# A two-layer decoder kernel: attention probabilities turned a step later, and half of layer 1's memory keys computed between the layers and a quarter inside layer 0's router

## The chip, the cores and the metric

The kernel runs on one core of a Trainium2 chip. The metric is device time in microseconds (us) for one call, the lower the better; the median of three runs stands for the kernel.

The engines are TensorE (PE in the profile; its weight loads are PEld), VectorE (DVE), ScalarE (ACT), GpSimd (POOL) and SyncE (SP), which issues the weight loads. Each runs its own list of instructions in order, and they wait for each other by semaphores.

## The reference, cut to what matters

Two layers (L = 2) over 256 tokens of width 1024, all in float32. In each layer:

```python
mix = hybrid_mixer(x, positions, w_in[l], ...)          # 4 latent + 6 forgetting + 6 dilated heads
x = layer_norm(ALPHA * x + mix, ln_mix_g[l], ln_mix_b[l])
# memory_cross_attention, 4 heads of 256:
q = to_heads(x @ xattn_w_q[l])
k, v = split(mem @ xattn_w_kv[l], 2)                    # mem doesn't depend on x or l
x = layer_norm(ALPHA * x + softmax(q k^T / 16) v @ xattn_w_o[l], ...)
gates = shared_group_router(x, router_w, router_bias)   # one group of four, two experts of it
x = layer_norm(ALPHA * x + moe_ffn(x, gates, ...))      # 16 experts
```

The memory keys are `mem @ xattn_w_kv[l][:, 0:1024]`. They depend on the memory and on the layer's weights alone, so they can be computed at any time before the cross-attention of their layer.

## The kernel before, in words

**Weights.** All weights come in one fixed order, `weight_stream` (L53): 168 blocks ("subs") for each layer, each of 128 partitions and up to 1024 elements. SyncE loads block i into a ring of 12 raw slots (L451) once VectorE is through with block i - 12. ScalarE writes the high part of the block into one of 4 slots, `split_hi` (L500, L504), after TensorE has freed that slot; VectorE writes what is left, `split_lo` (L506, L509). A product of TensorE is three matmuls: high by high, high by low, low by high (L1557 to L1559). A block of keys (`columns`, L1592) is 24 matmuls of 256 columns; a block of width 512 (`rows`, L1578) is 12 of 512 columns, one of the input projections 12 of 384 to 416.

**Jobs and banks.** Every projection is a job with a pair of PSUM banks (table at L276). A job may open when the job that held its pair is evacuated (L1569). A is the latent projection, FQ, FK, FV the forgetting heads, DQ, DK, DV the dilated heads, UQ and UKV the second latent step, MK0 and MK1 the memory keys (feature chunks 0 to 3 and 4 to 7), MV0 and MV1 the memory values, WO0 and WO1 the output projection, XQ, XO the cross-attention's projections, RT the router, U and D the experts.

**The head loop.** After UKV, `for s in range(HEADS + 3)` (PE L1975, ACT L858, DVE L1408) runs 19 steps over 16 heads. `slots` (L405) deals the 29 blocks from FQ's third to WO0's third over the steps. In step s the engines do, each in this order:

- TensorE: the blocks of step s; the value products of heads s-4 and s-3 together (even s from 4); turn head s-2's probabilities; scores of head s-1; turn queries and keys of head s.
- ScalarE: high halves for the blocks of step s+1; copies of finished jobs (DK, MK0, MK1 and others); copy of queries and keys of head s (L732); exponentials of head s-1 (L746); high part of the output (L754).
- VectorE: low halves for the blocks of step s+1 (L509); copies of DV and MV0 (L1047); scaled and masked scores with their maximum, and nmx (L1063, L1066), of head s-1; copy of the turned probabilities of head s-2 (L1097); sum's reciprocal and normalised probabilities of head s-1 (L1085, L1089; dilated heads are weighted by dilcount first, L1082); low part of the output (L1107).

The last six heads (dilated) go in pairs: scores and maxima of two heads in every second step. p_sb and pT have two slots. GpSimd rotates dq and dk in the early steps (L600 to L606); in layer 0 it builds the dilated masks before.

**Between the layers.** At the end of layer 0 TensorE adds up the experts' outputs (`scatter`, L1864). VectorE then adds and normalises token tile 0 and tile 1 (L1144, L1161). TensorE turns each tile when it is ready. In the meantime it runs fill matmuls whose result nobody reads (`keep_busy`, L1657): 20, then 5, then 11 (L1917, L1923, L1933). ScalarE and VectorE split the first two blocks of A ahead of that.

**The router.** After the cross-attention TensorE scores the tokens. It runs 6 fill matmuls while it waits for tile 1 (L2058), then 11 in `gather` (L1814) while VectorE picks the groups (L1207), ending in `ing` (L1233), and 2 more before the selected tokens are gathered.

## Time and profile before

| what | value |
|---|---|
| median of 3 runs | 820.36 us (818.98 to 822.27) |
| profiled execution, its own time | 822.08 us |
| span of the profiled execution | 820.5 us |
| mean granted TensorE clock | 0.990 |
| PE busy | 797.2 us, 97% |
| PEld busy | 688.0 us, 84% |
| DVE busy | 634.1 us, 77% |
| ACT busy | 508.5 us, 62% |
| POOL busy | 78.4 us, 10% |
| read from HBM | 175.18 MB, 215 GB/s over the span |
| chain that ended last | PE 81%, DVE 10%, ACT 4%, issue 2%, DMA 2% |

The span goes from the first to the last instruction. A matmul counts as busy from its start to the end of its drain, and the next one starts before that end; so the distance of two starts is what a matmul costs in a dense row, and not its own duration. In a row of the timeline the first number is the start, the second the time to the end of the last instruction that the row merges (x2: two of them), and a bracket names the idle time before and what ended it.

### The profile page before, as it was taken

To read this page: it belongs to the slowest core of one execution; us is meant where nothing else is said; L and a number is where in the kernel's file an instruction comes from. 1 tells how busy PE (TensorE), PEld (TensorE's weight loads), DVE (VectorE), ACT (ScalarE), POOL (GpSimd) and SP (SyncE) were. 2 spreads that over 40 slices of the span, in tenths; PEclk is the share of its full clock that TensorE was granted. 3 is DMA by queue.
4 is the path that set the end of the run, shared out by engine and by line. 5 is a ranking of instruction groups with operands and counts; after the bars stand their busy time and mean duration, and the time that the engine had idled before them with its cause. 6 is when DMAs were issued, how large, how long until landed. Compare 5 with 4: busy or idle time off the path is not lost.

```text
span 820.5 us, 12140 instructions
## 1 busy us (share of the span) xinstructions
PE 797.2 (97%) x4364; PEld 688.0 (84%) x4364; DVE 634.1 (77%) x1110; ACT 508.5 (62%) x804; POOL 78.4 (10%) x150
## 2 busy tenths in 40 slices
PE   7899999999999999999999999999999999999995
PEld 7899897789877888888899989877998788888884
DVE  5657868785658999999765586786846699999995
ACT  4755554554546788888555555554454567888873
POOL 3148200020000000000011350000200000000000
PEclk9999999999999999999999999999999999999998
DMA  8954443475334799999755644336643439999951
GB/s 289 344 182 155 144 135 130 139 228 157 105 126 134 246 368 367 364 370 374 259 150 146 209 142 154 105 129 204 209 129 99 145 120 342 367 369 364 370 209 52
DMA packets 122095, 177.06 MB, mean 216 GB/s; under 512 B 10177, under 2 KB 90577, under 8 KB 122033
## 3 DMA queue, kind: packets, MB, share of 16 engines
q1 hardware_dynamic: 120048, 169.56, 62.0%
q0 software_dynamic: 1984, 6.70, 2.9%
q8 instruction: 36, 0.59, 0.3%
q14 instruction: 27, 0.21, 0.1%
HBM read 175.18 MB, written 1.05 MB: 215 GB/s over the span
## 4 chain that ended last, share of the span: by engine, by line
PE 81%; DVE 10%; ACT 4%; issue 2%; DMA 2%; SPq 0%; POOL 0%; DVEq 0%; ACTq 0%; POOLq 0%
PE bank L1557 22%; PE bank L1559 22%; PE bank L1558 22%; DVE w_split L509 3%; DMA raw<-in_w_in_dram 2%; PE bank L1660 2%; PE bank L1724 2%; PE bank L1765 2%; PE bank L1870 2%; DVE xg_lo L1496 1%; ACT w_split L504 1%; PE bank L1756 1%; PE bank L1735 1%; PE bank L1713 1%; PE bank L1785 1%
## 5 line engine op out<-in xcount | busy, mean ns | idle before, releaser
L509 DVE TENSOR_TENSOR w_split<-raw,w_split 128x1024 fp32r<-128x1024 f32 (+3 forms) x336 | 386.0, 1173 | 69.8 <-ACT w_split L504 63.6
L504 ACT ACTIVATE w_split<-raw 128x1024 fp32r<-128x1024 f32 (+3 forms) x336 | 335.4, 1010 | 103.7 <-PE bank L1559 86.2
L1557 PE MATMUL bank<-w_split,xg_hi 128*128 128x512 f32 x256 | 102.9, 402 | 0.0
L1559 PE MATMUL bank<-w_split,xg_lo 128*128 128x512 f32 x256 | 100.1, 391 | 0.0
L1558 PE MATMUL bank<-w_split,xg_hi 128*128 128x512 f32 x256 | 99.9, 390 | 0.0
L1557 PE MATMUL bank<-w_split,xT_hi 128*128 128x384 f32 (+2 forms) x224 | 77.9, 348 | 3.1 <-DVE w_split L509 2.3
L1559 PE MATMUL bank<-w_split,xT_lo 128*128 128x384 f32 (+2 forms) x224 | 76.5, 341 | 0.0
L1558 PE MATMUL bank<-w_split,xT_hi 128*128 128x384 f32 (+2 forms) x224 | 76.2, 340 | 0.0
L1559 PEld LDWEIGHTS bank<-w_split,xg_lo 128*128 128x128 f32 x256 | 48.0, 188 | 10.3
L1557 PEld LDWEIGHTS bank<-w_split,xg_hi 128*128 128x128 f32 x256 | 48.1, 188 | 9.5 <-DVE xg_lo L1496 0.6
L1558 PEld LDWEIGHTS bank<-w_split,xg_hi 128*128 128x128 f32 x256 | 48.2, 188 | 9.0
L1557 PE MATMUL bank<-w_split,mixT_hi 128*128 128x512 f32 x128 | 51.9, 405 | 2.0 <-DVE w_split L509 1.9
L1559 PE MATMUL bank<-w_split,mixT_lo 128*128 128x512 f32 x128 | 50.0, 391 | 0.0
L1558 PE MATMUL bank<-w_split,mixT_hi 128*128 128x512 f32 x128 | 50.0, 390 | 0.0
L1559 PE MATMUL bank<-w_split,aT_lo 128*128 128x512 f32 x128 | 49.8, 389 | 0.0
L1557 PE MATMUL bank<-w_split,aT_hi 128*128 128x512 f32 x128 | 49.8, 389 | 0.0
L1558 PE MATMUL bank<-w_split,aT_hi 128*128 128x512 f32 x128 | 49.8, 389 | 0.0
L732 ACT ACTIVATE qkT<-bank 66x512 f32<-66x512 f32 (+2 forms) x26 | 15.5, 595 | 53.4 <-PE bank L1693 39.6
L1557 PEld LDWEIGHTS bank<-w_split,xT_hi 128*128 128x128 f32 x224 | 42.7, 191 | 4.3 <-issue 2.6
L1558 PEld LDWEIGHTS bank<-w_split,xT_hi 128*128 128x128 f32 x224 | 42.6, 190 | 0.2
L1559 PEld LDWEIGHTS bank<-w_split,xT_lo 128*128 128x128 f32 x224 | 42.5, 190 | 0.1
L746 ACT ACTIVATE p_sb<-p_sb,nmx 128x128 f32<-128x128 f32 x64 | 28.6, 447 | 19.1 <-DVE nmx L1066 18.8
(314 smaller groups left out, 1550.9 us busy)
## 6 DMA issues: line engine op xcount, KB each, us to landing
raw<-in_expert_w_gate_dram SPq DMA_DIRECT2D x128, 256.0 KB, 5.8
raw<-in_expert_w_up_dram SPq DMA_DIRECT2D x128, 256.0 KB, 7.8
raw<-in_expert_w_down_dram SPq DMA_DIRECT2D x64, 512.0 KB, 7.8
raw<-in_xattn_w_kv_dram SPq DMA_DIRECT2D x32, 512.0 KB, 4.1
raw<-in_w_in_dram SPq DMA_DIRECT2D x40, 384.0 KB, 4.0
raw<-in_w_mix_out_dram SPq DMA_DIRECT2D x16, 512.0 KB, 3.8
raw<-in_xattn_w_q_dram SPq DMA_DIRECT2D x16, 512.0 KB, 3.4
raw<-in_xattn_w_o_dram SPq DMA_DIRECT2D x16, 512.0 KB, 5.5
```

Source lines behind the costliest of these rows:

```text
L504: nc.scalar.activation(w_hi[:, i % SPL, 0:w], raw[:, i % RAW, 0:w], ACT.Copy).then_inc(hi_ready, 1)
L509: nc.vector.tensor_tensor(w_lo[:, i % SPL, 0:w], raw[:, i % RAW, 0:w], w_hi[:, i % SPL, 0:w].bitcast(F32), ALU.subtract).then_inc(lo_ready, 1)
L732: nc.scalar.activation(qkT[0:d, qk_slot(h), :], B_QK[0:d, :], ACT.Copy).then_inc(qkT_ready.sem, n)
L746: nc.scalar.activation(p_sb[:, h % 2, sl], src, ACT.Exp, bias=nmx[:, h, t:t + 1], scale=scale, accum_out=acc[:, h, t:t + 1]).then_inc(e_re ...
L1496: nc.vector.tensor_tensor(xg_lo[:, f, :, :].rearrange("p g s -> p (g s)"), bank[XG_BANKS[f]][:, :], xg_hi[:, f, :, :].rearrange("p g s -> ...
L1557: nc.tensor.matmul(o, lhs[0], rhs[0], start=first, stop=False, skip_group_check=shared)
L1558: nc.tensor.matmul(o, lhs[0], rhs[1], start=False, stop=False, skip_group_check=shared)
L1559: return nc.tensor.matmul(o, lhs[1], rhs[0], start=False, stop=last, skip_group_check=shared)
L1660: nc.tensor.matmul(bank[7][:, :], ones[:, :], memT_hi[:, 0:2, :].rearrange("p k t -> p (k t)"), start=True, stop=True)
L1724: ins = nc.tensor.matmul(o[:, t * T:(t + 1) * T], qTx[:, 2 * g + c_, t * P:(t + 1) * P], kTx[:, 2 * g + c_, :], start=c_ == 0, stop=c_ == 1)
L1765: ins = nc.tensor.matmul(value_bank(h)[:, dblk * T:(dblk + 1) * T], vx[:, c_, f * P:(f + 1) * P], pT[:, h % 2, c_ * T:(c_ + 1) * T], start ...
L1870: ins = nc.tensor.matmul(bank[2 * t + h][:, :], selT[:, g, t * P:(t + 1) * P], v[:, g, 512 * h:512 * h + 512], start=g == 0 and v is y_hi, ...
```

## The change

1. **Probabilities turned a step later.** The head loop has 20 steps. TensorE turns head s-3's probabilities in step s and makes the value products from step 5 on. VectorE's order in a step becomes: low halves; normalise head s-2; copy of the turned probabilities of s-3; maxima of s-1; output. Three slots of probabilities (`probs`) and two of turned ones take the place of p_sb and pT. The exponentials of dilated heads no longer write their sums.
2. **Layer 1's keys.** MK0 and MK1 exist in layer 0 only. In layer 1 ME1 (4 blocks, keys' chunks 4 to 7) stands between the layers in place of the 36 fill matmuls. MH0 (2 blocks, chunks 0 and 1) is computed into bank 7 in layer 0's router in place of the 6 and the 11 fills; its split parts have a buffer of their own (`early`), so it takes no turn in the ring of 4. The result is kept in `kept` and copied into kTx in layer 1. MH1 (2 blocks, chunks 2 and 3) stays in layer 1's head loop.
3. `slots` is a list for each layer: layer 0 gets one step more with one block, layer 1 has 23 blocks, one a step after the first two steps. ScalarE and VectorE split ME1 ahead at the end of layer 0, in place of two blocks of A. UKV uses bank pair 1, and from MV0 on layer 1 swaps pairs 0 and 1.

Cut to its core (index and signature changes that follow from it are left out):

```diff
@@ weight_stream @@
+        if l:
+            subs += [(l, "ME1", j) for j in range(4)]
...
-                         ("MK0", range(4)), ("MK1", range(4)), ("MV0", range(4)), ...
+                         ("MK0", range(0 if l else 4)), ("MK1", range(0 if l else 4)), ("MH1", range(2 if l else 0)), ("MV0", range(4)), ...
...
+            if name == "RT" and l + 1 < n_layers:
+                subs += [(l + 1, "MH0", 0)]
             subs += [(l, name, j) for j in js]
+            if name == "RT" and l + 1 < n_layers:
+                subs += [(l + 1, "MH0", 1)]
@@ build @@
-        slots = [3, 2, 2] + [2, 1] * 4 + [1, 2] * 2 + [1] * 4
+        slots = [[3, 2, 2] + [2, 1] * 4 + [1, 2] + [1] * 7] + [[3, 2] + [1] * 18] * (L - 1)
...
+        def free_turns(h):
+            return h - 2 if h < HEADS else max(h - 1, HEADS)
...
+            if i in turn_of:
+                act.wait_ge(split_free, slot_freed(i))
+            nc.scalar.activation(halves_of(i)[0][:, 0:w], raw[:, i % RAW, 0:w], ACT.Copy).then_inc(hi_ready, 1)
@@ scalar @@
-                if h >= 2:
-                    act.wait_ge(pt_done.sem, pt_done.at(l, h - 1))
+                if h >= 3:
+                    act.wait_ge(pt_done.sem, pt_done.at(l, free_turns(h)))
...
-                if l == 0:
-                    split_hi(act, first)
+                split_hi(act, first)
                 turn_x(l, "XT0", 0)
...
+                if l:
+                    act.wait_ge(split_free, free_at(index[l, "UKV", 0]))
+                    nc.scalar.activation(kTx[:, 0:2, :], kept[:, :, :], ACT.Copy).then_inc(keys_moved.sem, 1)
+                    keys(l, "ME1", 4)
...
                 for j in range(2):
                     split_hi(act, index[l, "RT", j])
+                if l + 1 < L:
+                    split_hi(act, index[l + 1, "MH0", 1])
...
+                if l + 1 < L:
+                    wait_job(l + 1, "MH0")
+                    nc.scalar.activation(kept[:, :, :], bank[7][:, :].rearrange("p (c t) -> p c t", c=2), ACT.Copy)\
+                        .then_inc(early_kept.sem, 1)
...
                 if l + 1 < L:
-                    for j in range(2):
-                        split_hi(act, index[l + 1, "A", j])
+                    for j in range(3):
+                        split_hi(act, index[l + 1, "ME1", j])
                 y_of(l, NG - 1)
+                if l + 1 < L:
+                    split_hi(act, index[l + 1, "ME1", 3])
@@ vector @@
-                for s in range(HEADS + 3):
+                for s in range(HEADS + VALUED):
                     for i in ahead_of[l][s]:
                         split_lo(dve, i)
...
+                    if 2 <= s < HEADS + 2:
+                        softmax_norm(l, s - 2)
+                    if TURNED <= s < HEADS + TURNED:
+                        evac_pT(l, s - TURNED)
                     for h in scored(s):
                         softmax_max(l, h)
-                    if in_pair(s - 1) and s % 2 == 0:
-                        softmax_norm(l, s - 1)
-                    if 2 <= s <= HEADS + 1:
-                        evac_pT(l, s - 2)
-                    if 1 <= s <= HEADS and not (in_pair(s - 1) and s % 2 == 0):
-                        softmax_norm(l, s - 1)
...
                 split_lo(dve, index[l, "XO1", 3])
+                if l + 1 < L:
+                    split_lo(dve, index[l + 1, "MH0", 0])
...
                 for j in range(2):
                     split_lo(dve, index[l, "RT", j])
+                if l + 1 < L:
+                    split_lo(dve, index[l + 1, "MH0", 1])
...
                 if l + 1 < L:
-                    for j in range(2):
-                        split_lo(dve, index[l + 1, "A", j])
+                    for j in range(3):
+                        split_lo(dve, index[l + 1, "ME1", j])
                 y_of(l, NG - 1)
+                if l + 1 < L:
+                    split_lo(dve, index[l + 1, "ME1", 3])
@@ tensor @@
+            def half_columns(l, name, j, b):
+                parts = sub_in(index[l, name, j])
+                for k in range(4):
+                    kc = 4 * j + k
+                    r = tuple(v[:, kc, :] for v in memT)
+                    for cb in range(2):
+                        lhs = tuple(v[:, k * T + cb * P:k * T + (cb + 1) * P] for v in parts)
+                        ins = product(b[:, cb * T:(cb + 1) * T], lhs, r, kc == 0 and cb == 0, kc == KC - 1 and cb == 1, shared=True)
+                ins.then_inc(split_free, 1)
+                return ins
...
-                keep_busy(11)
+                if l + 1 < L:
+                    half_columns(l + 1, "MH0", 1, bank[7])
+                else:
+                    keep_busy(11)
...
+                if l + 1 < L:
+                    pe.wait_ge(early_kept.sem, early_kept.at(l, 1))
                 keep_busy(2)
...
                 if l:
-                    keep_busy(20)
+                    gemm(index[l, "ME1", 0])
+                    gemm(index[l, "ME1", 1])
...
                 if l:
-                    keep_busy(5)
                     pe.wait_ge(end_half.sem, end_half.at(l - 1, 1))
...
-                    keep_busy(11)
+                    gemm(index[l, "ME1", 2])
+                    gemm(index[l, "ME1", 3])
...
-                for s in range(HEADS + 3):
+                for s in range(HEADS + VALUED):
                     for i in turns[l][s]:
                         gemm(i)
-                    if s >= 3 and (s - 3) % 2 == 1:
-                        head_values(l, s - 3)
-                    if 2 <= s <= HEADS + 1:
-                        head_turn(l, s - 2)
+                    if s >= VALUED and (s - VALUED) % 2 == 1:
+                        head_values(l, s - VALUED)
+                    if TURNED <= s < HEADS + TURNED:
+                        head_turn(l, s - TURNED)
...
                 score_tokens(0, 0, "XT0c")
-                keep_busy(6)
+                if l + 1 < L:
+                    half_columns(l + 1, "MH0", 0, bank[7])
+                else:
+                    keep_busy(6)
```

TURNED is 3 and VALUED is 4.

## Rows read from the trace of the kernel before

**Rows 1.** Windows: busy time and instructions of each engine, PE clock, DMA.

```profile
475.00:500.00 25.00, 24.51 (x169) 22.20 (x168) 20.66 (x55) 13.16 (x33) 8.08 (x8) 1.00 0.43 147
```

**Rows 2.** Timeline, PE: start us, us, what; ends of the head stages.

```profile
51.59 0.33 PE L1557 MATMUL bank<-w_split,xT_hi 128*128 128x384 f32 x1
...
154.34 0.50 PE L1557 MATMUL bank<-w_split,mixT_hi 128*128 128x512 f32 x1
...
454.12 0.33 PE L1557 MATMUL bank<-w_split,xT_hi 128*128 128x384 f32 x1
...
556.52 0.50 PE L1557 MATMUL bank<-w_split,mixT_hi 128*128 128x512 f32 x1
```

**Rows 3.** Timeline, DVE and ACT, layer 1, head 0 and the next two blocks.

```profile
466.67 0.17 DVE L1066 TENSOR_SCALAR nmx<-mx 128x2 f32<-128x2 f32 x1
...
467.77 1.57 ACT L504 ACTIVATE w_split<-raw 128x768 fp32r<-128x768 f32 x2
...
468.10 0.55 DVE L1089 TENSOR_SCALAR p_sb<-p_sb,ri 128x128 f32<-128x128 f32 x2
...
468.64 1.83 DVE L509 TENSOR_TENSOR w_split<-raw,w_split 128x768 fp32r<-128x768 f32 x2
```

**Rows 4.** Timeline, ACT, DVE and PE, layer 1, around 548 us.

```profile
547.09 1.04 ACT L504 ACTIVATE w_split<-raw 128x1024 fp32r<-128x1024 f32 x1
...
548.16 1.23 DVE L509 TENSOR_TENSOR w_split<-raw,w_split 128x1024 fp32r<-128x1024 f32 x1 [0.20 <-ACT w_split L504]
...
549.53 0.47 PE L1557 MATMUL bank<-w_split,mixT_hi 128*128 128x512 f32 x1 [0.96 <-DVE w_split L509]
```

**Rows 5.** Timeline, PE, layer 1, first and next after 96 products.

```profile
586.19 0.28 PE L1557 MATMUL bank<-xT_hi,w_split 128*128 128x256 f32 x1
...
597.71 0.38 PE L1724 MATMUL bank<-kTx,qTx 128*128 128x256 f32 x1
```

**Rows 6.** Timeline, DVE, layer 1, dilated heads.

```profile
522.10 0.28 DVE L1063 CUSTOM_DVE_ANT_0 p_sb<-bank,dilmask 128x128 f32<-128x128 f32 x1
...
523.64 0.17 DVE L1066 TENSOR_SCALAR nmx<-mx 128x2 f32<-128x2 f32 x1
...
543.24 1.28 DVE L1047 COPY vx<-bank 128x512 f32<-128x512 f32 x2
...
549.30 0.28 DVE L1082 CUSTOM_DVE_ANT_0 p_sb<-p_sb,dilcount 128x128 f32<-128x128 f32 x1
...
550.64 0.55 DVE L1097 COPY pT<-bank 128x384 f32<-128x384 f32 x1
```

**Rows 7.** Timeline, DVE, while GpSimd rotates.

```profile
75.36 0.90 DVE L1066 TENSOR_SCALAR nmx<-mx 128x2 f32<-128x2 f32 x1
...
474.54 1.91 DVE L1089 TENSOR_SCALAR p_sb<-p_sb,ri 128x128 f32<-128x128 f32 x2
```

**Rows 8.** Timeline, PE and DVE, between the layers.

```profile
407.46 0.69 DVE L1113 SCALAR_TENSOR_TENSOR xs<-xs,bank 128x512 f32<-128x512 f32 x1 [0.98 <-PE bank L1870]
...
408.93 4.70 PE L1660 MATMUL bank<-memT_hi,ones 128*128 128x512 f32 x20
...
416.59 2.75 PE L1660 MATMUL bank<-memT_hi,ones 128*128 128x512 f32 x11
...
419.18 0.35 PE L1557 MATMUL bank<-w_split,xT_hi 128*128 128x416 f32 x1
```

**Rows 9.** Timeline, PE and DVE, layer 0's router, and one window.

```profile
247.25 1.32 PE L2064 MATMUL bank<-ident,xs 128*128 128x128 f32 x8 [1.41 <-DVE xs L1161]
...
251.00 4.34 PE L1660 MATMUL bank<-memT_hi,ones 128*128 128x512 f32 x11
...
254.07 0.17 DVE L1233 TENSOR_TENSOR ing<-rt 128x8 fp32r<-128x8 f32 x1
...
255.19 0.17 PE L1818 MATMUL bank<-ing,upto 128*128 128x4 f32 x1
...
252.00:256.00 4.00, 4.00 (x16) 3.22 (x14) 2.43 (x14) 3.97 (x6) 0.00 (x0) 0.65 0.86 239
```

More of the change, by code:

```diff
@@ L40 @@
 SPL = 4
+TURNED, VALUED = 3, 4
 class Signal:
@@ L123, in free_at, with slot_of, slot_freed @@
         return SPL + i + 1
+    ring = [i for i, key in enumerate(stream) if key[1] != "MH0"]
+    turn_of = {i: n for n, i in enumerate(ring)}
+    def slot_of(i):
+        return turn_of[i] % SPL
+    def slot_freed(i):
+        n = turn_of[i] - SPL
+        return free_at(ring[n]) if n >= 0 else SPL
     with ExitStack() as ctx:
@@ L222, in build @@
         assert m5 <= used
+        early, m2b = sb("early", [P, 2, 2, 1024], F32R, at=m0)
+        assert m2b <= m2 and m5 <= used - 2 * T * 4
+        kept, _ = sb("kept", [P, 2, T], at=used - 2 * T * 4)
         rt, m6 = sb("rt", [P, 16, TT * NE], at=m2)
@@ L281, in build, with left_out, pair_in, held_by @@
         job = {name: n for n, (name, _, _, _) in enumerate(jobs)}
-        pair = {name: k for name, _, _, k in jobs}
-        held_by = {}
-        for n, (name, _, _, k) in enumerate(jobs):
-            held_by[name] = next((m for m, _, _, k_ in reversed(jobs[:n]) if k_ == k), None)
-        evac_a = np.cumsum([a for _, a, _, _ in jobs]).tolist()
-        evac_v = np.cumsum([v for _, _, v, _ in jobs]).tolist()
+        def left_out(l):
+            return ("MK0", "MK1") if l else ("ME1", "MH1")
+        def pair_in(l, name, k):
+            return 1 - k if l and k < 2 and job[name] >= job["MV0"] else k
+        pair = [{name: pair_in(l, name, k) for name, _, _, k in jobs} for l in range(L)]
+        def held_by(l, name):
+            return next((m for m, _, _, _ in reversed(jobs[:job[name]]) if m not in left_out(l) and pair[l][m] == pair[l][name]), None)
+        def evacuations(l, k):
+            return np.cumsum([0 if j[0] in left_out(l) else j[k] for j in jobs]).tolist()
+        evac_a, evac_v = ([evacuations(l, k) for l in range(L)] for k in (1, 2))
         XG_BANKS = (0, 6, 7, 2, 3, 1, 5, 4)
@@ L475, in pieces_of @@
                     return [(row.rearrange("p (k n) -> p k n", k=4), feat(router_w)[:, 4 * j:4 * j + 4, :])]
-                src, c0 = {"MK0": (xattn_w_kv, 0), "MK1": (xattn_w_kv, 512), "MV0": (xattn_w_kv, 1024),
+                if name in ("MH0", "MH1"):
+                    c0 = 0 if name == "MH0" else 256
+                    return [(row.rearrange("p (k n) -> p k n", k=4), feat(xattn_w_kv[l])[:, 4 * j:4 * j + 4, c0:c0 + 256])]
+                src, c0 = {"MK0": (xattn_w_kv, 0), "MK1": (xattn_w_kv, 512), "ME1": (xattn_w_kv, 512), "MV0": (xattn_w_kv, 1024),
                            "MV1": (xattn_w_kv, 1536), "WO0": (w_mix_out, 0), "WO1": (w_mix_out, 512),
@@ L497, in _, with halves_of @@
             sp.wait_ge(out_sent, 48)
+        def halves_of(i):
+            if stream[i][1] == "MH0":
+                return early[:, 0, stream[i][2], :], early[:, 1, stream[i][2], :]
+            return w_hi[:, slot_of(i), :], w_lo[:, slot_of(i), :]
         def split_hi(act, i):
@@ L1607, in _ @@
             xT, memT, mixT, latT = (xT_hi, xT_lo), (memT_hi, memT_lo), (mixT_hi, mixT_lo), (latT_hi, latT_lo)
-            KINDS = {"MK0": (columns, memT), "MK1": (columns, memT), "XQ0": (columns, xT), "XQ1": (columns, xT),
+            KINDS = {"MK0": (columns, memT), "MK1": (columns, memT), "ME1": (columns, memT), "XQ0": (columns, xT), "XQ1": (columns, xT),
                      "MV0": (rows, memT, 512), "MV1": (rows, memT, 512), "WO0": (rows, mixT, 512),
@@ L1995, in _ @@
                 ready(l, "XQ0")
-                ready(l, "MK1")
+                ready(l, "MH1" if l else "MK1")
+                pe.wait_ge(keys_moved.sem, keys_moved.at(l, 0))
                 head_scores(l, HEADS)
```

204 lines of the change are left out of this document (115 added, 89 removed), and 4 rows, old and new, of the table jobs.

## Prediction, made before the changed kernel was run

> **What bounds the kernel now.** I read the times by stage first, then the marks on TensorE in the two head stages, then one step of the head loop in order of time over all engines. In a stretch of the head loop TensorE is busy for 24.5 of 25 us while VectorE (20.7) and ScalarE (13.2) are not [rows 1], so today nearly everything that leaves TensorE there shortens the time. A head stage, from the first block of FQ after UKV to the first block of WO1, takes 102.4 us in layer 1 and 102.75 us in layer 0 [rows 2]. The reader should next look at the step itself: the scaled maximum nmx ends at 466.84; ScalarE's exponentials hold it until 467.77, when it may split the next weight block; VectorE normalises until 468.64 and then takes the low halves [rows 3]. That chain is short today because normalising runs beside ScalarE's split. It is already TensorE's bound once per layer: ScalarE splits at 547.09, VectorE takes the low half at 548.16, and TensorE, idle for 0.96 us, starts at 549.53 [rows 4].
>
> **What leaves and what is added on TensorE.** Price of the 256-column products: 96 of them (24 per block, four blocks of XQ0 and XQ1) run from 586.19 to 597.71, 11.52 us, so 0.120 each and 2.88 a block [rows 5]. Layer 1's head stage loses MK0 and MK1 (8 blocks) and gets MH1 (2 blocks): 6 x 2.88 = 17.3 us less. Were TensorE the bound to the end, it would fall to 85.1 us. As a weighed rule, the Trainium skill (TensorE: Matmul & The Clock Gate, Back-to-back issue gap) gives N/2.4 + 2.5 ns, 109 ns for 256 columns; by it the 17.3 would be 15.7. The row is 10% longer and the sum goes by the row.
>
> **The new ring in the head loop (the main term).** VectorE's order in step s was: low halves of the blocks of step s+1, maximum of head s-1, turned copy of s-2, normalise s-1. It becomes: low halves, normalise s-2, turned copy of s-3, maximum of s-1. ScalarE's order is kept: high halves for s+1, queries and keys of s, exponentials of s-1. So from one maximum to the next everything now stands in one line: exponentials, then ScalarE's high half (queued behind them), then VectorE's low half (first in its step, waiting for that), then normalising and turned copy behind the low half, then the maximum. Durations for a 768-wide block: 0.93 from nmx to the split, 0.80 high (1.57 for two), 0.92 low (1.83 for two), 0.74 normalise (0.55 and the reciprocal) [rows 3], 0.50 turned copy, 0.86 maximum (half of 1.71 for a pair) [rows 6]: 4.75 us a step. A 1024-wide block takes 1.06 and 1.14 [rows 4, 6]: 5.23. A second block of the same step adds its low half, 0.92 or 1.14. In the dilated heads a pair takes two steps: exponentials without accumulators 0.73 (estimate: 0.93 less two reads of 0.1), output copy 0.27 (estimate), high 1.06, twice (low 1.14, count and normalise 1.34, copy 0.50), both maxima 1.71 [rows 6]: 9.7 us.
>
> **Layer 1.** nmx of head 0 ends 12.7 us into the stage [rows 2, 3]; nothing before it changes on TensorE. The moved copies (kept keys, two of ME1, about 1.7 us on ScalarE) delay the next splits, but head 1's block is split about when TensorE asks for it; I take 0, at most 0.5. Step 2 has no turned copy: 4.25. Steps 3 to 9: 7 x 4.75 = 33.2. Output copies in ScalarE's queue: 0.8. Step 10 has a 1024 block and the copy of DV, about 0.95 (from 1.2 for the wider MV0 [rows 6]): 6.2. Step 11, two maxima: 6.1. Two pairs: 19.5. Maximum of head 15 is then at 82.7. Behind it: 0.73 + 0.27 + 1.06 + 1.14, copy of MV0 1.2, normalise 1.34, copy 0.50 = 6.2 until head 13's turned copy; then TensorE alone has two value products (0.8 each), two turns (0.4 each; estimates at 0.1 us a short matmul) and the last two WO0 blocks (as many columns as a block of keys, 2.85 each), 8.1. Sum 97.0 us, against 85.1 by TensorE's work alone: the ring binds, and about 12 of the 17.3 us are not gained.
>
> **Layer 0.** Work on TensorE is unchanged, 20 steps instead of 19. Steps 2 to 11 carry the same blocks as before. Up to step 3 TensorE binds: nmx of head 2 would end at 75.53 undisturbed, 23.9 into the stage [rows 7], less 0.3 for the turn that leaves: 23.6. Then the ring: step 4 (two 768 blocks) 5.7, 5 (one) 4.8, 6 (768 and 1024) 6.2, 7 (1024, copy of DV) 6.2, 8 (two 1024) 6.6, 9 and 10 (one) 5.2 and 5.5, 11 (two, two maxima) 7.2, with the output copies: 47.4, so 71.0 at head 11; two pairs 19.5; tail 14.3: 104.8 against 102.75, +2.0. The turn's later place can give back at most the 1 to 2 us of waits inside a layer [rows 4].
>
> **GpSimd on the ring.** While it rotates dq and dk, VectorE's in-place operations stretch: a normalising pair took 1.91 instead of 0.55 [rows 3, 7], and an nmx 0.90 instead of 0.17 [rows 7]. With two such pairs and one nmx a layer that is 2 x 1.36 + 0.73 = 3.5 us; today TensorE's block work hides most. On a ring that binds it counts. Bounds 0 and 3.5 (about 5 in layer 0, where the dilated masks are built too); VectorE idles more in the new step, so I take 1.5 in each layer. The Trainium skill (Trainium Architecture — The Big Picture, What this means for kernel authors) calls the shared port of the two an exclusive lock; by that rule no part of it would be shared, which speaks for the upper end; the stretched row agrees.
> So layer 1: 97.0 + 1.5 = 98.5, **-3.9**. Layer 0: 106.3, **+3.5**.
>
> **Between the layers.** 36 fill matmuls go: 20 from 408.93, the rest until 419.18, when A starts [rows 8]. In their place stand four blocks of ME1, 11.5 us. By order: scatter ends 408.9; two blocks 5.8 to 414.7; transposes of token tile 0 to 415.5; tile 1's cannot end before x, 416.6 today; two blocks 5.8: 422.4, which is +3.2. VectorE has four 1024-wide low halves (1.14) where it had two of 832: the last stands behind the y copies and puts the first addition, which waited 0.98 for TensorE, from 407.46 to about 408.05 [rows 8], and that chain sets x: +0.6. A's own splits fit beside the blocks. Together **+3.8**, bounds +2.5 and +4.5.
>
> **Router of layer 0.** MH0's first block (2.88) takes the place of 6 fills and of the 1.41 us in which TensorE waits for x: it fits in the 3.05 us up to 247.25. The second replaces 11 fills from 251.00. Its splits lie in idle time of ScalarE and VectorE before the tile is added (the early buffer waits for no slot), its copy from bank 7 is done before the selection. The clock there is 0.65 of 2.4 GHz, so part of those fills ran at 1.2 GHz, behind the idle 1.41 us; they end only at 255.19 though VectorE had ing at 254.24 [rows 9]. With work in the gap the clock may stay at 2.4 GHz; then the block ends at 253.9: **-0.9**. If it falls all the same, the block has 9% more columns than the fills: +0.3. SP's queue gets as many loads (8 keys blocks of 512 KB before and after), earlier; layer 1's A blocks arrive behind ME1 in a ring of 12 that is full at this point. No wait on a load; 0.
>
> **Sum.** +3.5 - 3.9 + 3.8 - 0.9 = +2.5 us. The profiled execution took 822.08 (span 820.5 and 1.6 around it), 1.7 above the median 820.36. It becomes 824.6, and against the median **822.9 us**. About 0.5% (4.1 us) is what a measurement of this kernel can tell from no change.
>
> **Rivals.**
> (a) TensorE stays the bound: ScalarE's split isn't held behind the exponentials, or my links overlap. For it: TensorE is busy for 24.5 of 25 us [rows 1], and every probability then has a step more. Against: the order of both queues. Layer 1 -17.3, waits of both layers -4, boundary +3.8, router -0.9: -18.4, 802.
> (b) The ring binds but links are shorter by half a microsecond a step, or layer 0 keeps its 102.7: -6 to -12, some 812.
> (c) Slower: GpSimd's rotations fall wholly on the ring, in both layers. Place: steps 2 to 6, VectorE's normalise and nmx. Price 3.5 in layer 1 and 5 in layer 0 instead of 1.5 each, +5.5: 828.4. It decides once more than 4.6 us of its delay in all (3 are in the forecast) are on the ring. TensorE's clock falling in the new gaps (under 1 us in each 4.75) would add to it.
> (d) Nothing but the boundary and router counts and the stages stay at today's length: +2.9, 823; not to be told from the forecast by the time, only by the waits.
>
> **How the numbers follow.** Forecast and (d) 0.42, (a) 0.16, (b) 0.14, (c) 0.28. Faster is (a) and (b), 0.30; within 0.5% 0.42; slower 0.28. The range leaves out (a) and the last of (c): 810 to 830. The likeliest case's own range is 817 to 825.
>
> **What would show it.** In layer 1's head stage: steps of about 4.8 us; VectorE's low half waiting for ScalarE's high half in each (about 1.7 us); TensorE waiting for w_split about a dozen times, its busy share near 87%; a stage of 97 to 100 us, in layer 0 104 to 107. A's first product 13.5 to 14.5 us after the scatter instead of 10.25. Clock near 1.00 where it was 0.65. I am wrong in the main step if TensorE doesn't wait for w_split there, or the stage is below 92 us.

## The result, and the profile after

| | kernel before | changed kernel |
|---|---|---|
| median of its runs, us | 821.32 (818.98 to 825.62) | **833.61** (831.56 to 835.45) |
| profiled execution, span, us | 822.08, 820.5 | 834.73, 832.7 |
| mean granted TensorE clock | 0.990 | 0.981 |
| head stage, layer 0, us | 102.75 | 111.72 |
| head stage, layer 1, us | 102.40 | 103.03 |
| end of layer 0's stage to start of layer 1's, us | 299.78 | 303.12 |

The ratio is 1.0143, 95% interval 1.0092 to 1.0194: the change makes the kernel slower, by 12.3 us. (The median of before has a fourth run here; the forecast started from 820.36.) The forecast was 822.9 us, range 810 to 830: outside, and the likeliest case was not the one that came.

The stages add up to the spans: +9.0 and +0.6 in the head stages, +3.3 between them, +1.8 behind layer 1's stage (its router stretch, which the change leaves alone: the granted clock was at half for 6.8 us there, 3.4 in the profile of before), -2.5 ahead of layer 0's stage (also left alone; TensorE waited 2.3 us for a split block there in the profile of before and not in this one): +12.2.

The windows of the changed kernel over its two head stages; columns are length, busy time (instructions) of PE, PEld, DVE, ACT and POOL, then PE clock, DMA share and GB/s:

```profile
core 0: us, PE busy (x) PEld busy (x) DVE busy (x) ACT busy (x) POOL busy (x), PEclk, DMA share, GB/s
49.07:160.79 111.72, 104.46 (x673) 91.50 (x672) 78.54 (x213) 55.20 (x114) 30.39 (x33) 0.97 0.40 133
463.91:566.94 103.03, 88.59 (x529) 74.01 (x527) 69.59 (x207) 49.00 (x109) 16.91 (x20) 0.97 0.35 113
```

In layer 1 TensorE is idle for 14.4 of 103 us, and the 17.3 us of key products that left have shortened nothing. In layer 0, with the work of before, it is idle for 7.3, and 3.5 us more of the stage count as busy than before (104.5 against 101): the same products at a lower clock, seen in the 0.97.

Who makes it wait: the waits of the changed kernel, from 49 to 567 us.

```profile
DVE w_split L568 <- ACT w_split L562: 69.8, 58, 3.9
ACT probs L804 <- DVE nmx L1143: 65.9, 23, 6.2
PE bank L1642 <- DVE w_split L568: 19.3, 14, 2.1
```

VectorE's low half waits for ScalarE's high half, which stands behind the exponentials in ScalarE's queue, and the exponentials wait for VectorE's maximum, which stands behind the low half in VectorE's. That is a ring of two engines; TensorE waits beside it for the low half. One turn of it in layer 1, VectorE first, then ScalarE, then TensorE:

```profile
487.33 0.17 DVE L1143 TENSOR_SCALAR nmx<-mx 128x2 f32<-128x2 f32 x1
489.28 0.96 DVE L568 TENSOR_TENSOR w_split<-raw,w_split 128x768 fp32r<-128x768 f32 x1 [1.78 <-ACT w_split L562]
490.35 0.55 DVE L1166 TENSOR_SCALAR probs<-probs,ri 128x128 f32<-128x128 f32 x2
490.81 0.55 DVE L1176 COPY probs<-bank 128x384 f32<-128x384 f32 x1
491.49 0.42 DVE L1140 CUSTOM_DVE_ANT_0 probs<-bank,causal 128x256 f32<-128x256 f32 x1
491.95 0.17 DVE L1143 TENSOR_SCALAR nmx<-mx 128x2 f32<-128x2 f32 x1
...
487.53 0.40 ACT L804 ACTIVATE probs<-probs,nmx 128x128 f32<-128x128 f32 x1 [3.05 <-DVE nmx L1143]
488.42 0.83 ACT L562 ACTIVATE w_split<-raw 128x768 fp32r<-128x768 f32 x1
...
490.29 0.44 PE L1642 MATMUL bank<-w_split,xT_hi 128*128 128x384 f32 x1 [1.40 <-DVE w_split L568]
```

From nmx to nmx 4.62 us, forecast 4.75 from [rows 3, 4, 6]; VectorE's low half waits 1.78, forecast 1.7; and nothing in the turn waits for TensorE. Three turns of layer 1 have this length; the others, with more copies, wider blocks or a rotation in them, are longer. One beside a rotation:

```profile
499.87 1.87 DVE L1166 TENSOR_SCALAR probs<-probs,ri 128x128 f32<-128x128 f32 x2
501.67 0.54 DVE L1176 COPY probs<-bank 128x384 f32<-128x384 f32 x1
502.79 0.79 DVE L1143 TENSOR_SCALAR nmx<-mx 128x2 f32<-128x2 f32 x1
...
499.60 1.02 POOL L658 TENSOR_TENSOR rot<-dk,cosb 128x384 f32<-128x384 f32 x1 [13.68 <-ACT dk L779]
502.56 0.99 POOL L661 TENSOR_TENSOR rot<-dk,cosb 128x384 f32<-128x384 f32 x1
```

This turn takes 6.83 us from the end of one nmx to the end of the next. Between the layers, the answer to [rows 8]: the last row of the scatter, the first of ME1, the transposes of token tile 1, A's first product.

```profile
414.62 0.39 PE L1980 MATMUL bank<-y_lo,selT 128*128 128x512 f32 x1
414.84 0.28 PE L1642 MATMUL bank<-memT_hi,w_split 128*128 128x256 f32 x1
...
422.07 1.32 PE L2038 MATMUL bank<-ident,xs 128*128 128x128 f32 x8 [0.44 <-DVE xs L1240]
...
428.97 0.35 PE L1642 MATMUL bank<-w_split,xT_hi 128*128 128x416 f32 x1
```

A starts 14.1 us behind the scatter instead of 10.25: +3.9.

Not all of the loss in the head stages lies in the turns. Of the 9.0 us in layer 0, 5.5 stand behind the last maximum (15.85 us against 10.4), where the extra step leaves TensorE nearly alone; the forecast had 3.9 of them in its sum.

### The profile page after: what moved, and what is told of

Its sections match the earlier page's. It is cut to its first block, busy times and chain, and to the rows that moved or that the text cites. A ratio compares the mean times of both kernels' runs of the same rounds, so it can differ in the third digit from the quotient of the medians.

```text
span 832.7 us, 12012 instructions
## 1 busy us (share of the span) xinstructions
PE 794.7 (95%) x4311; PEld 683.6 (82%) x4311; DVE 632.2 (76%) x1110; ACT 506.3 (61%) x782; POOL 75.8 (9%) x150
## 4 chain that ended last, share of the span: by engine, by line
PE 76%; DVE 15%; ACT 5%; issue 3%; DMA 1%; DVEq 0%; SPq 0%; ACTq 0%
PE bank L1642 22%; PE bank L1643 21%; PE bank L1644 21%; DVE w_split L568 5%; ACT w_split L562 2%; PE bank L1827 2%; PE bank L1870 2%; ACT probs L804 1%; DVE probs L1140 1%; DVE xg_lo L1578 1%; PE bank L1861 1%; PE bank L1980 1%; DVE probs L1166 1%; PE bank L1890 1%; DVE xs L1192 1%
## 5 line engine op out<-in xcount | busy, mean ns | idle before, releaser
L804 ACT ACTIVATE probs<-probs,nmx 128x128 f32<-128x128 f32 x64 | 27.5, 448 | 66.3 <-DVE nmx L1143 65.9
L1642 PE MATMUL bank<-w_split,mixT_hi 128*128 128x512 f32 x128 | 52.7, 412 | 4.3 <-DVE w_split L568 4.2
L1644 PEld LDWEIGHTS bank<-w_split,xg_lo 128*128 128x128 f32 x256 | 48.0, 188 | 10.2
L1642 PEld LDWEIGHTS bank<-w_split,xg_hi 128*128 128x128 f32 x256 | 48.1, 188 | 9.4 <-DVE xg_lo L1578 0.5
L1643 PE MATMUL bank<-w_split,mixT_hi 128*128 128x512 f32 x128 | 50.9, 398 | 0.0
L1642 PE MATMUL bank<-memT_hi,w_split 128*128 128x256 f32 x112 | 33.1, 296 | 2.4 <-DVE w_split L568 2.4
```

The source lines that it names most:

```text
L804: nc.scalar.activation(probs_of(h)[:, sl], src, ACT.Exp, bias=nmx[:, h, t:t + 1], scale=scale, **total)\
L1642: nc.tensor.matmul(o, lhs[0], rhs[0], start=first, stop=False, skip_group_check=shared)
L1643: nc.tensor.matmul(o, lhs[0], rhs[1], start=False, stop=False, skip_group_check=shared)
L1644: return nc.tensor.matmul(o, lhs[1], rhs[0], start=False, stop=last, skip_group_check=shared)
```

## The experiments

One table holds what the profiles of all kernels show; the sections below refer to it. "Idle" is TensorE's, the stage less its busy time; "end" is the part behind the maximum of head 15. All in us.

| kernel | median | layer 0: stage, idle, end | layer 1: stage, idle, end |
|---|---|---|---|
| before | 821.32 | 102.75, 1.8, 10.4 | 102.40, 1.8, 10.4 |
| changed | 833.61 | 111.72, 7.3, 15.9 | 103.03, 14.4, 15.8 |
| turned later alone | 837.1 | 111.79, 7.3, 15.9 | 110.75, 7.6, 15.9 |
| keys moved alone | 813.56 | 102.18, 1.5, 10.2 | 90.33, 5.2, 10.2 |
| changed, maximum first | 820.53 | 106.11, 4.4, 15.0 | 92.93, 6.9, 15.0 |
| changed, normalise last | 819.54 | 106.11, 4.4, 15.0 | 96.74, 9.1, 16.6 |
| changed, high halves ahead | 819.81 | 106.20, 5.0, 13.9 | 92.02, 6.8, 13.9 |
| changed, high products first | 826.3 | 107.57, 5.8, 14.3 | 99.84, 11.1, 14.3 |
| changed, small rotations | 827.42 | 108.00, 5.1, 15.9 | 99.79, 12.5, 14.6 |
| changed, gap filled | 832.21 | 110.54, 6.7, 14.6 | 101.83, 11.5, 14.6 |
| keys, high halves ahead | 821.06 | 107.58, 6.2, 10.1 | 93.27, 7.9, 10.1 |
| keys, high products first | 808.16 | 100.51, 0.5, 9.0 | 88.56, 4.6, 9.0 |
| keys, scores first | 807.63 | 101.67, 1.1, 10.2 | 87.68, 2.8, 10.2 |
| keys, both | **805.0** | 99.99, 0.2, 9.0 | 85.57, 2.2, 9.0 |

### Each half of the change alone

The head loop alone, on the kernel before:

```diff
+TURNED, VALUED = 3, 4
...
-                    for h in scored(s):
-                        softmax_max(l, h)
-                    if in_pair(s - 1) and s % 2 == 0:
-                        softmax_norm(l, s - 1)
-                    if 2 <= s <= HEADS + 1:
-                        evac_pT(l, s - 2)
-                    if 1 <= s <= HEADS and not (in_pair(s - 1) and s % 2 == 0):
-                        softmax_norm(l, s - 1)
+                    if 2 <= s < HEADS + 2:
+                        softmax_norm(l, s - 2)
+                    if TURNED <= s < HEADS + TURNED:
+                        evac_pT(l, s - TURNED)
+                    for h in scored(s):
+                        softmax_max(l, h)
...
-                    if 2 <= s <= HEADS + 1:
-                        head_turn(l, s - 2)
+                    if TURNED <= s < HEADS + TURNED:
+                        head_turn(l, s - TURNED)
```

> The kernel before with the new head loop alone (probabilities turned a step later, new order on VectorE, four blocks more of ring-free work: 20 steps), and no key moved. Ring theory: both layers then look like layer 0 of the changed kernel, +9 us each with nothing gained between: kernel at 836 to 842 us, 15 to 21 over the kernel before. Rival, the cost lies with the moved keys (boundary, banks, slots): at most 4 us over the kernel before.

Measured: 837.1 us, ratio to before 1.0174 (1.0134 to 1.0214), +9.0 and +8.4 us in the two stages. The new head loop is the whole loss and more.

The keys alone, on the changed kernel (layer 1's 23 blocks over 19 steps; the lines of `slots` are left out):

```diff
-TURNED, VALUED = 3, 4
+TURNED, VALUED = 2, 3
...
-                    if 2 <= s < HEADS + 2:
-                        softmax_norm(l, s - 2)
-                    if TURNED <= s < HEADS + TURNED:
-                        evac_pT(l, s - TURNED)
                     for h in scored(s):
                         softmax_max(l, h)
+                    if in_pair(s - 1) and s % 2 == 0:
+                        softmax_norm(l, s - 1)
+                    if TURNED <= s < HEADS + TURNED:
+                        evac_pT(l, s - TURNED)
+                    if 1 <= s <= HEADS and not (in_pair(s - 1) and s % 2 == 0):
+                        softmax_norm(l, s - 1)
```

> The changed kernel with the head loop of before (turned two steps after, maximum right behind the low halves, 19 steps) and the keys moved. Ring theory: layer 1's head stage loses most of 17.3 us on TensorE, 102.4 to 87 to 92; boundary +3.9, router -0.9, layer 0's stage as before: kernel at 808 to 815 us. Rival, VectorE and ScalarE bound layer 1's stage in the old order too once the blocks are gone: stage 97 to 102, kernel 820 to 825 us.

Measured: 813.56 us, ratio 0.9899 (0.9866 to 0.9933), layer 1's stage 90.33: inside the expected 87 to 92. Moving the keys pays 12.1 us in the stage, against 3.9 between the layers. The trace also says what most of the idle time left there (5.2 us) is: for 3.6 us TensorE waits to turn head s-2 until it is normalised.

### The ring cut in three places

VectorE's maximum first, then turned copy, then normalise:

```diff
-                    if 2 <= s < HEADS + 2:
-                        softmax_norm(l, s - 2)
+                    for h in scored(s):
+                        softmax_max(l, h)
                     if TURNED <= s < HEADS + TURNED:
                         evac_pT(l, s - TURNED)
-                    for h in scored(s):
-                        softmax_max(l, h)
+                    if 2 <= s < HEADS + 2:
+                        softmax_norm(l, s - 2)
```

> The changed kernel with one edit: in each step of the head loop VectorE takes the maximum of head s-1 right behind the low halves, then the turned copy of s-3, then normalises s-2 (the changed kernel had normalise, copy, maximum). Ring theory: from one maximum to the next there remain exponentials 0.93, high half 0.80, low half 0.92, maximum 0.86 = 3.5 us, less than the 4.1 us that TensorE's own work of a step takes, so TensorE stops waiting for w_split in most steps; layer 1's head stage falls from 103.0 to 88 to 93 us, layer 0's from 111.7 to 100 to 104, the kernel to 806 to 815 us. Rival, the extra step itself costs (its emptier end, GpSimd's rotations, TensorE's clock): the stages shorten by 2 us each at most and the kernel stays at 828 to 833 us.

Measured: 820.53 us, ratio to before 0.9989 (0.9973 to 1.0005). Layer 1's stage fell by 10.1 us to 92.9, as the ring theory said; layer 0's to 106.1, two more than it said, and the kernel is 5.5 us above the expected range. VectorE in one step:

```profile
486.25 0.96 DVE L568 TENSOR_TENSOR w_split<-raw,w_split 128x768 fp32r<-128x768 f32 x1 [0.66 <-ACT w_split L562]
488.18 0.29 DVE L1140 CUSTOM_DVE_ANT_0 probs<-bank,causal 128x128 f32<-128x128 f32 x1 [0.97 <-PE bank L1816]
488.86 0.17 DVE L1143 TENSOR_SCALAR nmx<-mx 128x2 f32<-128x2 f32 x1
```

The maximum now waits 0.97 us for TensorE's scores: TensorE bounds this step. The rest that did not come back is in the dilated pairs (10.5 us a pair as in the changed kernel in layer 1; normalising stands last and TensorE waits 0.87 for it, then 0.5 to 1.0 for the low half) and in the end.

Normalise taken out of the ring, the copy left in:

```diff
-                    if 2 <= s < HEADS + 2:
-                        softmax_norm(l, s - 2)
...
                     for h in scored(s):
                         softmax_max(l, h)
+                    if 2 <= s < HEADS + 2:
+                        softmax_norm(l, s - 2)
```

> The changed kernel, VectorE's step in the order low halves, turned copy, maximum, normalise (one link, normalising, taken out of the ring, the copy left in). Ring theory: 0.93 + 0.80 + 0.92 + 0.50 + 0.86 = 4.0 us from maximum to maximum, about TensorE's own 4.1: between the changed kernel and the one with the maximum first, nearer to the latter: layer 1's stage 93 to 96, kernel 820 to 825 us. Rival, the step's order does not matter so finely and only the maximum behind the low half frees TensorE: 829 to 834 us.

Measured: 819.54 us, ratio 0.9978 (0.9965 to 0.9992); in layer 1 the turn that has no wait for TensorE and no rotation beside it takes 3.96 us from the end of one nmx to the end of the next, expected 4.0:

```profile
481.53 0.82 DVE L1143 TENSOR_SCALAR nmx<-mx 128x2 f32<-128x2 f32 x1
...
486.14 0.17 DVE L1143 TENSOR_SCALAR nmx<-mx 128x2 f32<-128x2 f32 x1
```

The stage is 96.7, 0.7 above its range, and the kernel 0.5 below its own; the clock fell in layer 1's end here (16.6 us, 15.0 in layer 0). So the lengths add as links of a ring: 4.62 with normalise and copy, 3.96 without the one, and below TensorE's own time without both.

The link on ScalarE cut, VectorE left as changed:

```diff
-                    for i in ahead_of[l][s]:
-                        split_hi(act, i)
...
+                    if s + 1 < HEADS + VALUED:
+                        for i in ahead_of[l][s + 1]:
+                            split_hi(act, i)
                     for h in scored(s):
                         exps(l, h)
```

> The changed kernel with one edit: ScalarE splits the high halves one step further ahead, ahead of the exponentials of the same step; VectorE's order is left as changed. Ring theory: the low half no longer waits for exponentials and high half, the ring is exponentials 0.93 (beside VectorE's low half 0.92), then normalise, copy, maximum 2.1: about 3.1 to 4.0 us a step, so TensorE bounds most steps again: stages as in the run with the maximum first, kernel 806 to 816 us. Rival, the cause is VectorE's or GpSimd's time alone and not the link through ScalarE: 828 to 834 us.

Measured: 819.81 us, ratio 0.9978 (0.9957 to 0.9998). Cutting at another engine gives the same 14 us back: what was too long was the circle, not VectorE's work. It is 4 us above the range: layer 0's stage, at 106.2, is 2 above its own; what the rest is stays open.

What none of the three cuts gives back is the end: 13.9 to 15.0 us (16.6 where the clock fell) against 10.2 with the keys alone. With the maximum first, layer 1's steps between the maxima of heads 0 and 11 are even shorter than with the keys alone, 44.3 us against 48.9. The pairs (21.0 for two, against 18.5) and the end take it back. So the extra step has a price of its own, apart from the ring.

### Is TensorE on the ring?

```diff
+                pe.wait_ge(hi_ready, hi_at(i))
+                for o, lhs, rhs, first, last in triples:
+                    other = (lhs[0], rhs[1]) if weights == 0 else (lhs[1], rhs[0])
+                    nc.tensor.matmul(o, lhs[0], rhs[0], start=first, stop=False, skip_group_check=True)
+                    nc.tensor.matmul(o, other[0], other[1], start=False, stop=False, skip_group_check=True)
                 pe.wait_ge(lo_ready, lo_at(i))
+                for o, lhs, rhs, first, last in triples:
+                    low = (lhs[1], rhs[0]) if weights == 0 else (lhs[0], rhs[1])
+                    ins = nc.tensor.matmul(o, low[0], low[1], start=False, stop=last, skip_group_check=True)
```

> The changed kernel, with TensorE taking the two thirds of every block's products that need only the high half of the weights first, and waiting for the low half behind them. Ring theory (the ring is on ScalarE and VectorE, TensorE only waits for it): steps among the causal heads stay at 4.6 us, only the pairs and the end, where VectorE waits 0.5 us for scores, shorten, and TensorE's clock falls less: layer 1's stage 97 to 101, kernel 824 to 831 us. Rival, the waits of 1.0 to 2.1 us for the low half are themselves the loss: 14 of them gone, kernel 812 to 820 us.

Measured: 826.3 us, layer 1's stage 99.8, both inside the range. The causal steps kept their 4.62 us although TensorE began their blocks with the high half (MH0's and MH1's are products of another function, which the edit leaves as it is); PE, then VectorE:

```profile
484.74 0.44 PE L1669 MATMUL bank<-w_split,xT_hi 128*128 128x384 f32 x1 [0.53 <-ACT w_split L562]
...
487.38 0.17 DVE L1143 TENSOR_SCALAR nmx<-mx 128x2 f32<-128x2 f32 x1
492.00 0.17 DVE L1143 TENSOR_SCALAR nmx<-mx 128x2 f32<-128x2 f32 x1
```

TensorE only waits for the ring there; its waits are not the loss. In the dilated pairs it was part of it: a pair falls from 10.5 to 9.7 us, which is the length that the forecast gave by counting VectorE and ScalarE alone.

### GpSimd

The kernel leaves out the rotation of five of the six dilated heads.

```diff
-                    rotate(l, q[:, :, :, :], q[:, :, :, :], DIL_H, 32, 1, 14 + 6 * n)
+                    rotate(l, q[:, :, 0:1, :], q[:, :, 0:1, :], 1, 32, 1, 14 + 6 * n)
```

> The changed kernel, GpSimd rotating only the first of the six dilated heads of dq and dk (the rotation of the other five is left out). GpSimd theory: VectorE's normalise at 1.87 instead of 0.55 and nmx at 0.80 to 0.88 instead of 0.17 lie wholly on the ring: layer 1's head stage 103.0 to 98.5 to 100, layer 0's 111.7 to 105 to 108 (with the slow TensorE stretch at 78 to 82 us gone as well), kernel 822 to 826 us. Rival, TensorE's work hides them as in the kernel before: 830 to 834 us.

Measured: 827.42 us, stages 108.0 and 99.8 (expected 105 to 108 and 98.5 to 100). Between the maxima of heads 0 and 11 the changed kernel's 62.2 and 53.5 us became 58.4 and 49.95: 3.8 and 3.5 us. The row that was 1.87:

```profile
490.57 0.55 DVE L1166 TENSOR_SCALAR probs<-probs,ri 128x128 f32<-128x128 f32 x2
```

Without the other rotations the steps come out nearly as the forecast had summed them without GpSimd: 58.4 against 58.3 us in layer 0, 49.95 against 50.6 in layer 1.

The kernel's time is 1.4 above the range though both stages are inside theirs. In the profile 2.1 us more than in the changed kernel's lie outside the stages. In layer 1 the clock fell in a pair (12.1 us instead of 10.5) and not in the end (14.6 instead of 15.8). No run separates these.

### TensorE's clock in the gap

In the changed kernel TensorE waits 2.12 us for the low half of the first WO0 block, and the next stretches run at half clock. Its timeline:

```profile
554.56 0.47 PE L1642 MATMUL bank<-w_split,mixT_hi 128*128 128x512 f32 x1 [2.12 <-DVE w_split L568]
```

And the windows of PE around it (length, busy, PEclk, DMA share, GB/s):

```profile
554.00:556.00 2.00, 1.44 (x7) 1.00 0.19 47
556.00:558.00 2.00, 2.00 (x6) 0.51 0.57 215
558.00:560.00 2.00, 2.00 (x12) 0.64 0.23 29
```

The block takes 4.09 us (554.56 to 558.65) where one at full clock takes 2.9. The experiment fills the gap with products that the block's first product overwrites:

```diff
                 if name == "WO0":
                     pe.wait_ge(o_lo.sem, o_lo.at(l, 2 * j + 2))
+                    if j == 0:
+                        open_job(l, name)
+                        for _ in range(8):
+                            nc.tensor.matmul(banks(l, name)[0][:, :], ones[:, :],
+                                             memT_hi[:, 0:2, :].rearrange("p k t -> p (k t)"), start=True, stop=True)
```

> The changed kernel with eight 512-column products (0.23 us each, 1.84 in all) written into the bank of the first WO0 block before its first real product, which overwrites them: they fill most of the 2.1 us in which TensorE waits there for the low half, once a layer. Clock theory (the fall of the granted clock behind that idle stretch lengthens the block from 2.9 to 4.1 us and the values from 0.87 to 1.25): the block takes 2.8 to 2.9 us, the part of the head stage behind the last maximum falls from 15.85 to 14.1 to 14.5 us in both layers, kernel 829.5 to 832 us. Rival, the clock falls there whatever TensorE does: 15.8 us, kernel unchanged at 833.6.

Measured: 832.21 us, both ends 14.6 instead of 15.85, each 0.1 or 0.2 above the expected range for it and for the kernel.

```profile
551.05 2.10 PE L1723 MATMUL bank<-memT_hi,ones 128*128 128x512 f32 x8
553.42 0.47 PE L1642 MATMUL bank<-w_split,mixT_hi 128*128 128x512 f32 x1 [0.27 <-DVE w_split L568]
556.35 0.87 PE L1866 MATMUL bank<-probs,dv 128*64 128x256 f32 x8
```

The block starts as late behind the last maximum as in the changed kernel (3.46 us) and takes 2.93 us. So a fall of the clock costs 1.25 us in a layer's end. Three kernels leave this wait of 2.1 us as it is (changed, turned later alone, small rotations): the clock fell behind it in five of their six ends, and in neither of the two filled ones. That speaks for idle TensorE as what lets it fall; the sixth end shows that it doesn't fall each time. Worth 2.4 us in the stages; the medians differ by 1.4, with overlapping runs.

A fall does not cost the same everywhere. Early in layer 0 the clock fell at 78.2 us in the changed kernel and not with the gap filled, and the turn there took 7.52 and 7.53 us from nmx to nmx: it cost nothing where TensorE is not on the ring.

### Better versions

All on the kernel with the keys moved and the old head loop. First the split ahead of the exponentials, as above:

> Keys moved, head loop of before (as in the run with the keys alone), and ScalarE's high halves split one step further ahead, ahead of the exponentials. If the link exponentials, high half, low half still costs in the old order: 1 to 3 us less than the keys alone, 810 to 813 us. Rival, the old order leaves nothing there and the split now holds the exponentials: 814 to 818 us.

Measured: 821.06 us, ratio to before 1.001 (0.9991 to 1.0029): 7.5 us worse than the keys alone, a miss beyond even the rival's range. VectorE's normalise in the keys alone, then here with ScalarE's queue:

```profile
481.47 0.17 DVE L1143 TENSOR_SCALAR nmx<-mx 128x2 f32<-128x2 f32 x1
482.70 0.17 DVE L1162 RECIPROCAL ri<-sm 128x2 f32<-128x2 f32 x1 [0.58 <-ACT probs L804]
```

```profile
482.95 0.17 DVE L1146 TENSOR_SCALAR nmx<-mx 128x2 f32<-128x2 f32 x1
484.80 0.17 DVE L1165 RECIPROCAL ri<-sm 128x2 f32<-128x2 f32 x1 [1.20 <-ACT probs L804]
...
483.05 0.84 ACT L562 ACTIVATE w_split<-raw 128x768 fp32r<-128x768 f32 x1
483.79 0.39 ACT L804 ACTIVATE probs<-probs,nmx 128x128 f32<-128x128 f32 x1
```

In the old order normalising s-1 needs the exponentials of the same step, and TensorE's turn needs it in the next. The split put 0.6 us more between maximum and normalise (from 1.06 to 1.68), and TensorE's waits for normalised probabilities rose from 0.5 and 3.6 us in the two layers to 4.8 and 6.7. What frees one ring lengthens another.

Then the products with the high half first:

> Keys moved with the head loop of before, and TensorE taking the products with the high half of the weights first in every block. Its waits for low halves in the head stages (0.8 us in layer 0, 1.2 in layer 1) and elsewhere go: 811 to 813.5 us. Rival, it gains nothing since nothing but these waits hangs on low halves and a block now frees its slot as late as before: 813 to 815 us.

Measured: 808.16 us, ratio 0.9831 (0.9793 to 0.9870), 3 us better than expected. 3.4 us of the gain are in the stages, where TensorE's waits for low halves are gone.

And the scores ahead of the turn:

```diff
-                    if TURNED <= s < HEADS + TURNED:
-                        head_turn(l, s - TURNED)
                     if scored(s):
                         head_scores(l, scored(s)[0])
+                    if TURNED <= s < HEADS + TURNED:
+                        head_turn(l, s - TURNED)
```

> Keys moved with the head loop of before, TensorE issuing in each step the scores of head s-1 ahead of the turn of head s-2. The turn waited 3.6 us in layer 1 for VectorE's normalising; with the scores (0.65 us) ahead of it, and the maximum that follows them earlier, half or more of it is covered: layer 1's stage 90.3 to 87.5 to 89, kernel 811 to 813 us. Rival, the turned copy comes later by as much and the values wait instead: 813 to 816 us.

Measured: 807.63 us, ratio 0.9843 (0.9805 to 0.9881), 3 us below the expected range; layer 1's stage 87.7, inside its own. The turn stands behind the scores and no longer waits:

```profile
482.56 0.39 PE L1817 MATMUL bank<-qkT 66*128 66x128 f32 x2
482.78 0.60 PE L1818 MATMUL bank<-qkT 66*128 66x256 f32 x2
483.21 0.49 PE L1842 MATMUL bank<-ident,probs 128*128 128x128 f32 x3
```

> Both edits of the two runs before it together (products with the high half first, scores ahead of the turn), on the kernel with the keys moved. If the two waits are independent: the sum of both gains, 809 to 812 us. Rival, they hide each other: no better than the better of the two.

Measured: **805.0 us**, ratio 0.9806 (0.9770 to 0.9842): 16 us under the kernel before, 28.6 under the changed one and 4 below the expected range. Both stages fell further, to 99.99 and 85.57, with 0.2 and 2.2 us of idle left. The stages of these two edits gave 3.4 and 3.2 us alone and 6.9 together, so the two waits are close to independent. The medians moved 5.4, 5.9 and 8.6; more of that than the stages show lies in the start of the kernel (layer 0's stage began anywhere from 48.1 to 51.6 us in these profiles) and in the clock of the router stretches, which these edits leave alone.

## Why the prediction was wrong

The step that failed is the sum of the two head stages: the ring was there, and three terms of the sum were sized too small. By its own steps:

- **The ring itself was right.** In layer 1's stage TensorE waits for w_split 10 times ("about a dozen") and is busy for 86% ("near 87%"), turns of 4.62 us against 4.75, low half waiting 1.78 against 1.7; three cuts, at VectorE's order and at ScalarE's, each gave 13 to 14 us back. That the 17.3 us of key products would mostly not be gained was right too, only not far enough: none was.
- **Between the layers: right.** +3.8 forecast, +3.9 measured, the same within 0.1 in every kernel with ME1 there. **Router: right**, -0.9 for -0.9 (100.85 to 99.91 us from the end of layer 0's stage to the router's ing products). The branch was luck: of the twelve kernels here with MH0 in the router six took 99.7 to 100.0 us, as forecast, and six 100.9 to 102.5, with the clock falling all the same (101.1 with the keys alone, 102.4 with the maximum first). The prediction had named it, at +0.3.
- **Outside the forecast's places**, +1.8 behind layer 1's stage and -2.5 ahead of layer 0's nearly cancel; neither stretch was changed.
- **The head stages: 10.0 us too short**, -0.4 forecast and +9.6 measured. Three terms were mis-sized.
  - "GpSimd on the ring ... I take 1.5 in each layer": 3.8 and 3.5, +4.3 in all. The prediction knew the upper bounds, 3.5 and about 5, and argued itself below them because VectorE idles more in the new step. It does, but its idle time lies ahead of the low half, while the stretched normalise and nmx stand behind it, with nothing between them and the next turn. On a ring that binds, slack elsewhere in the step covers nothing. In layer 0 a late nmx (0.88) also put ScalarE's copy of dk late, and TensorE waited 1.94 us; with the small rotations that wait is gone. This was rival (c)'s mechanism, in its place; its own time, 828.4, lacks the next two terms.
  - "Two pairs 19.5": 21.0, +1.5 a layer. A pair was counted over VectorE and ScalarE alone; the trace of layer 1 has VectorE waiting 0.49 us for TensorE's scores in each, and 0.15 and 0.12 for its turn. With TensorE started earlier a pair took 9.7, as forecast.
  - The end, 14.3: 15.85, +1.55 a layer, of which 1.25 is the clock at half speed behind a wait of 2.1 us. Clock was priced at nothing in the forecast and left to a half sentence in rival (c).

  These make 10.4; the turns, 0.13 shorter than forecast, take some of it back.
- **The chances.** Rival (c) had 0.28, and its condition (more than 4.6 us of GpSimd's delay on the ring) was met with 7.3. The range ended at 830 because its worst case added one mis-sized term to a sum in which three had the same sign. Two of them, the clock and the waits for TensorE in the pairs, had no price in it at all.

## What to carry to other kernels

When a change takes work off the bounding engine, walk one step of the loop from a signal back to the same signal through all queues and add up the links: an item placed behind a waiting one joins the circle even though its engine is half idle. Then price every known disturbance on that circle at its full length, since on a ring slack elsewhere covers nothing, and price what idle time does to TensorE's clock where TensorE is on the path. An extra step also lengthens the end of the loop, apart from any ring. Before turning data a step later to gain slack, ask which item should stand first behind the wait; here exchanging two issues on TensorE did more than the extra step.

## What the runs showed of the hardware

- The clock falls behind some waits and not behind others of the same length. In the head stages of the changed kernel it fell to half four times. Behind waits of 1.94, 2.11 and 2.12 us the next 12 products took 3.41 us (2.2 at full clock), 4.12 and 4.09 (2.9 at full clock); behind one of 1.69 us, 24 products took 4.5 us (3.0 at full clock). Waits of 1.59, 1.73 and 1.74 were not followed by a fall. With the gap filled, waits of 1.58 and 1.77 were, and one of 1.95 was not. With small rotations a wait of 2.12 was followed by a block of 2.91, some 20 us behind another fall, but with the gap filled two falls were 14 us apart. With the normalise last a wait of 1.43 was followed by a block of 4.50 in layer 1 and of 2.90 in layer 0. What tells these cases apart stays open; no run was made for it. A saving of a microsecond in the profile can thus be the clock alone.
- GpSimd lengthens only some of VectorE's instructions. While it rotated, the in-place TENSOR_SCALAR pair took 1.87 instead of 0.55 and the two-column nmx 0.79 instead of 0.17; the copy out of the bank took 0.54 as ever. The low half, 768 wide and 0.96 us alone, took from 0.94 to 1.76 us beside GpSimd: at most 1.07 beside the rotations of dq and dk in the changed kernel, but 1.50 twice in its layer 0 while the dilated masks were built, and 1.76 in the kernel before and 1.75 with the normalise last beside a rotation. The Trainium skill (SBUF — State Buffer, Who interferes with whom) names VectorE's instructions with two inputs in that memory among those that contend with a GpSimd instruction that reads it. The low half is one, and the rows agree in part: beside some of GpSimd's instructions it stretched by up to 0.8 us, beside others not at all.
